# One upward tile per group of the small expert items multiplied as fp32 from where it landed

## The reference

```
logits = t @ router_w + router_b            # 256 tokens, 8 experts
top_vals, top_idx = top_k(logits, 2);  top_w = softmax(top_vals)
for e in range(8):
    y = (silu(t @ w_gate[e]) * (t @ w_up[e])) @ w_down[e]     # 1024 -> 3584 -> 1024
    out += gates[:, e] * y
```

## Time and profile before

| what | us |
|---|---|
| median of 3 runs | 2671.87 (2670.59 to 2681.54) |
| the profiled execution | 2670.39 |
| its span in the profile | 2668.6 |
| the mixture's stretch in it, about | 1647 to 2648 |

### The profile page before, as it was taken

How to read it: one execution, slowest core, us unless ns; L and a number is a source line. 1 busy time by engine, 2 the same in 40 slices (tenths; PEclk the granted TensorE clock), 3 DMA queues, 4 the chain that set the end, 5 groups by cost and what they waited for, 6 DMA issues and landing times.

```text
span 2668.6 us, 45484 instructions
## 1 busy us (share of the span) xinstructions
PE 2522.3 (95%) x17582; PEld 2135.5 (80%) x17601; DVE 2020.8 (76%) x1962; ACT 1497.9 (56%) x1519; POOL 89.3 (3%) x82
## 2 busy tenths in 40 slices
PE   8999999999999999999999999998899899888987
PEld 7888898888889898888889987776787678666855
DVE  6666877666666866667666756989888998998898
ACT  5443524445443515445446734678767776786676
POOL 6000006000000000000000000000000000000000
PEclk9999999999999999999999999999999999999998
DMA  8665313555564314564565413999999999999993
GB/s 280 191 183 178 117 35 127 189 189 175 190 208 144 101 35 158 189 200 159 189 189 156 149 47 120 381 349 362 366 349 343 366 366 347 351 371 334 326 367 142
DMA packets 342893, 601.45 MB, mean 225 GB/s; under 512 B 11984, under 2 KB 180816, under 8 KB 342608
## 3 DMA queue, kind: packets, MB, share of 16 engines
q1 hardware_dynamic: 335264, 590.85, 64.6%
q10 hardware_dynamic: 7472, 8.35, 0.9%
HBM read 598.11 MB, written 1.05 MB: 225 GB/s over the span
## 4 chain that ended last, share of the span: by engine, by line
DMA 34%; PE 34%; DVE 18%; DVEq 7%; ACT 4%; issue 2%; another core or an unknown queue 0%; ACTq 0%; SPq 0%; PEld 0%; PEldq 0%
DMA raw<-in_ffn_w_down 12%; DVE wlo L316 12%; PE ps L567 6%; DMA raw<-in_w_in 6%; DVEq L318 6%; DMA raw<-in_moe_w_up 5%; DMA work<-in_moe_w_gate 4%; PE ps L591 4%; PE ps L570 3%; ACT whi L312 3%; PE ps L2983 3%; PE ps L856 2%; PE ps L3027 2%; PE ps L2988 1%; DMA raw<-in_moe_w_gate 1%
## 5 line engine op out<-in xcount | busy, mean ns | idle before, releaser
L316 DVE TENSOR_TENSOR wlo<-raw,whi 128x2048 fp32r<-128x2048 f32 (+1 forms) x394 | 901.9, 2289 | 183.3 <-ACT whi L312 172.3
L312 ACT CAST whi<-raw 128x2048 fp32r<-128x2048 f32 (+1 forms) x394 | 751.4, 1909 | 380.9 <-DMA raw<-in_ffn_w_down 142.6
L567 PE MATMUL ps<-xboth,whi 128*128 128x512 f32 x1680 | 420.8, 392 | 0.0
L2983 PE MATMUL ps<-whi,xboth 128*128 128x512 f32 x1344 | 352.7, 398 | 5.1 <-issue 3.9
L567 PEld LDWEIGHTS ps<-xboth,whi 128*128 128x128 f32 x1680 | 305.3, 189 | 57.1
L2983 PEld LDWEIGHTS ps<-whi,xboth 128*128 128x128 f32 x1344 | 246.3, 188 | 59.0 <-issue 7.8
L316 DVE TENSOR_TENSOR wlo<-U,whi 128x2048 fp32r<-128x2048 f32 x112 | 256.2, 2287 | 25.2 <-ACT whi L312 18.3
L2988 PE MATMUL ps<-wlo,xboth 128*128 128x512 f32 x896 | 248.0, 399 | 15.1 <-DVE wlo L316 12.8
L312 ACT CAST whi<-U 128x2048 fp32r<-128x2048 f32 x112 | 213.7, 1912 | 54.1 <-DMA U<-in_moe_w_up 44.1
L570 PEld LDWEIGHTS ps<-xboth,wlo 128*128 128x128 f32 x1680 | 229.2, 190 | 16.4
L570 PE MATMUL ps<-xboth,wlo 128*128 128x256 f32 x1680 | 234.2, 282 | 0.0
(11 more groups left out here) (586 smaller groups left out, 3738.9 us busy)
## 6 DMA issues: line engine op xcount, KB each, us to landing
raw<-in_moe_w_gate SPq DMA_DIRECT2D x58, 1024.0 KB, 6.2
raw<-in_moe_w_up SPq DMA_DIRECT2D x56, 1024.0 KB, 6.8
U<-in_moe_w_up SPq DMA_DIRECT2D x56, 1024.0 KB, 6.8
U<-in_moe_w_down SPq DMA_DIRECT2D x56, 1024.0 KB, 6.4
raw<-in_ffn_w_gate SPq DMA_DIRECT2D x55, 1024.0 KB, 5.4
raw<-in_ffn_w_up SPq DMA_DIRECT2D x55, 1024.0 KB, 5.4
raw<-in_ffn_w_down SPq DMA_DIRECT2D x55, 1024.0 KB, 5.0
work<-in_moe_w_gate SPq DMA_DIRECT2D x54, 1024.0 KB, 6.5
```

Of the source, the lines that this page charges most:

```text
L312: act.copy(whi[:, n % SPLIT, 0:width], buf[:, 0:width]).then_inc(hi_ready[n % RAW], 1)
L316: dve.tensor_tensor(wlo[:, n % SPLIT, 0:width], buf[:, 0:width], whi[:, n % SPLIT, 0:width], ALU.subtract).then_inc(split_ready[n % SPLIT], 1)
L567: pe.matmul(ps[:, first_bank + b, :], whi[:, n % SPLIT, c * GW + b * P:c * GW + (b + 1) * P], xboth[:, c].rearrange("p a t -> p (a t)"), s ...
L2983: pe.matmul(dst, part[:, rows, xhalf(q)], whi[:, (m + k) % SPLIT, c * EW:(c + 1) * EW], start=(rows == 0 and part is xhi), stop=False)
```

## The change

In groups 1 to 6 of each small item the second upward tile (u1, called whole) gets no high and no low part. TensorE multiplies it as fp32 straight from its slot, with `x_whole`, an fp32 copy of the lower half of the gathered rows of 64 tokens (four blocks of 128 x 64) that ScalarE makes with four more activations in `gather_hi`. That is 24 of the 336 tiles. Its four fp32 matmuls go to the upper 64 rows of bank 6 and signal `whole_done`. The slot is given free by ScalarE after it has waited for `whole_done` and copied the low rows of up. The places of `whi` and `wlo` are counted over the tiles that are split (`count`, `place`), and `ahead` names the tile that goes into a place next: four tiles later rather than three where a whole tile lies between. So VectorE's list has five subtractions between two `turned`: `refill` for a0 now makes d0's part, for a1 d1's, for u0 that of the next a0, for u1 nothing, for d0 that of the next a1, for d1 that of the next u0.

```
-        def split_hi(act, n, width=TILE, landed=16, slot_of=raw_slot):
+        def split_hi(act, n, width=TILE, landed=16, slot_of=raw_slot, place=None):
...
-            act.copy(whi[:, n % SPLIT, 0:width], buf[:, 0:width]).then_inc(hi_ready[n % RAW], 1)
+            act.copy(whi[:, n % SPLIT if place is None else place, 0:width], buf[:, 0:width]).then_inc(hi_ready[n % RAW], 1)
...
+        x_whole = mt(4 * FEW).rearrange("p (c t) -> p c t", c=4)
+        f["whole_done"] = f["pool_u0"]
...
+        WHOLE = [ITEM_TILES + 6 * g + 3 for g in range(EN - 1)]
+
+        def parts_plan(n):
+            body = n + 4
+
+            def whole(m):
+                return m >= body and (m - body) % (2 * ITEM_TILES) in WHOLE
+
+            def count(m):
+                rounds, rest = divmod(max(m - body, 0), 2 * ITEM_TILES)
+                return m - rounds * len(WHOLE) - sum(w < rest for w in WHOLE)
+
+            def place(m):
+                return count(m) % SPLIT
+
+            def ahead(m):
+                t = m + SPLIT
+                while whole(t) or count(t) < count(m) + SPLIT:
+                    t += 1
+                return t
...
+            def as_it_came(m, dst):
+
+                buf, landed, _ = slot_of(m)
+                take(pe, landed, 16)
+                for c in range(C // 2):
+                    mm = pe.matmul(dst[0:FEW], x_whole[:, c, :], buf[:, c * EW:(c + 1) * EW], start=False,
+                                   stop=(c == C // 2 - 1), skip_group_check=True)
+                mm.then_inc(f["whole_done"], 1)
...
                 for k in range(2):
                     begin(k)
+                    if whole(m + k):
+                        as_it_came(m + k, dst)
+                        continue
...
-                    take(act, tile_done[(m + 1) % SPLIT])
-                    low_copy(6, "up_low")
-                    if m + 1 + SPLIT < end:
-                        split_hi(act, m + 1 + SPLIT, slot_of=slot_of)
+                    if whole(m + 1):
+                        take(act, f["whole_done"])
+                        low_copy(6, "up_low")
+                        act.sem_inc(slot_of(m + 1)[2], 1)
+                    else:
+                        take(act, tile_done[place(m + 1)])
+                        low_copy(6, "up_low")
+                        split_after(m + 1, end)
...
             def gather_hi(bank, b, q):
+                if q and b == 1:
+                    for c in range(4, C):
+                        act.activation(x_whole[:, c - 4, :], four(bank)[:, c % 4, 0:FEW], ACT.Copy, scale=moe_gain(c))
...
             def refill(m, end):
-                if m < end:
-                    dve.wait_ge(hi_ready[m % RAW], 1)
-                    split_lo(dve, m, slot_of=slot_of)
+                if not whole(m) and ahead(m) < end:
+                    dve.wait_ge(hi_ready[ahead(m) % RAW], 1)
+                    split_lo(dve, ahead(m), slot_of=slot_of, place=place(m))
```

More of the change, by code:

```diff
@@ L311, in split_hi, with split_lo @@
             act.sem_clear(here)
-            act.copy(whi[:, n % SPLIT, 0:width], buf[:, 0:width]).then_inc(hi_ready[n % RAW], 1)
-        def split_lo(dve, n, width=TILE, slot_of=raw_slot):
+            act.copy(whi[:, n % SPLIT if place is None else place, 0:width], buf[:, 0:width]).then_inc(hi_ready[n % RAW], 1)
+        def split_lo(dve, n, width=TILE, slot_of=raw_slot, place=None):
             buf, _, free_ = slot_of(n)
-            dve.tensor_tensor(wlo[:, n % SPLIT, 0:width], buf[:, 0:width], whi[:, n % SPLIT, 0:width],
-                              ALU.subtract).then_inc(split_ready[n % SPLIT], 1)
+            at = n % SPLIT if place is None else place
+            dve.tensor_tensor(wlo[:, at, 0:width], buf[:, 0:width], whi[:, at, 0:width],
+                              ALU.subtract).then_inc(split_ready[at], 1)
             dve.drain().then_inc(free_, 1)
@@ L542, in build, with take_split @@
         PASSES = ((whi, 0), (wlo, 0), (whi, 1))
-        def take_split(pe, n):
-            take(pe, split_ready[n % SPLIT])
+        def take_split(pe, n, place=None):
+            take(pe, split_ready[n % SPLIT if place is None else place])
         def wide_fresh(pe, n, first_bank):
@@ L2910, in blocks_of @@
             return ps[:, bank, :].rearrange("p (k t) -> p k t", t=P)
+        WHOLE = [ITEM_TILES + 6 * g + 3 for g in range(EN - 1)]
[13 more added lines that the diff above has]
+                return t
+            assert (2 * ITEM_TILES - len(WHOLE)) % SPLIT == 0
+            return whole, place, ahead
         def moe_stream(sp, n, l):
@@ L2962, in moe_tensor @@
             first_tiles = range(n, n + SPLIT)
+            slot_of = moe_slots(n)
+            whole, place, _ = parts_plan(n)
             def upper(m):
@@ L2982, in by_token @@
                         for part in ((xhi,) if q else (xhi, xlo)):
-                            pe.matmul(dst, part[:, rows, xhalf(q)], whi[:, (m + k) % SPLIT, c * EW:(c + 1) * EW],
+                            pe.matmul(dst, part[:, rows, xhalf(q)], whi[:, place(m + k), c * EW:(c + 1) * EW],
                                       start=(rows == 0 and part is xhi), stop=False)
@@ L2987, in by_token @@
                         rows = k * C // 2 + c
-                        mm = pe.matmul(dst, xhi[:, rows, xhalf(q)], wlo[:, (m + k) % SPLIT, c * EW:(c + 1) * EW],
-                                       start=False, stop=(rows == C - 1))
-                    mm.then_inc(tile_done[(m + k) % SPLIT], 1)
+                        mm = pe.matmul(dst, xhi[:, rows, xhalf(q)], wlo[:, place(m + k), c * EW:(c + 1) * EW],
+                                       start=False, stop=(rows == C - 1 or (c == C // 2 - 1 and whole(m + k + 1))))
+                    mm.then_inc(tile_done[place(m + k)], 1)
             def add_low(low, whole, bank):
@@ L3026, in downs @@
                             for part in ((hh,) if q else (hh, hl)):
-                                pe.matmul(ps[:, s, :], part[:, 2 * k + b, :], whi[:, (m + k) % SPLIT, cols_of(b, s)],
+                                pe.matmul(ps[:, s, :], part[:, 2 * k + b, :], whi[:, place(m + k), cols_of(b, s)],
                                           start=False, stop=False, skip_group_check=True)
@@ L3031, in downs @@
                         for b in range(2):
-                            mm = pe.matmul(ps[:, s, :], hh[:, 2 * k + b, :], wlo[:, (m + k) % SPLIT, cols_of(b, s)],
+                            mm = pe.matmul(ps[:, s, :], hh[:, 2 * k + b, :], wlo[:, place(m + k), cols_of(b, s)],
                                            start=False, stop=(final and k == 1 and b == 1), skip_group_check=True)
-                    mm.then_inc(tile_done[(m + k) % SPLIT], 1)
+                    mm.then_inc(tile_done[place(m + k)], 1)
                 if final:
@@ L3119, in moe_scalar, with split_after @@
             slot_of = moe_slots(n)
+            whole, place, ahead = parts_plan(n)
+            def split_after(m, end):
+                if ahead(m) < end:
+                    split_hi(act, ahead(m), slot_of=slot_of, place=place(m))
             def next_split(m, end):
-                take(act, tile_done[m % SPLIT])
-                if m + SPLIT < end:
-                    split_hi(act, m + SPLIT, slot_of=slot_of)
+                take(act, tile_done[place(m)])
+                split_after(m, end)
             def low_copy(bank, low):
@@ L3262, in item @@
             def item(m, q, i, end, last=False):
-                m += SPLIT
                 for g in range(1, EN):
@@ L3336, in moe_vector @@
             for k in range(4):
-                refill(n + SPLIT + k, open_end)
+                refill(n + k, open_end)
             make_hid(0, 0)
@@ L3347, in moe_vector @@
             turned(1)
-            refill(end - 1, end)
+            refill(end - 1 - SPLIT, end)
             for s in range(2):
```

7 lines of the change are left out of this document (3 added, 4 removed).

## The result

The changed kernel takes 2637.53 us (median of 4 runs, 2636.47 to 2637.74); the kernel before, run beside it, 2676.46 us (2670.59 to 2681.54). The ratio is 0.9861, 95% interval [0.9848, 0.9875]: about 37 us faster (the two medians lie 38.9 us apart). The forecast was 2645.3 us, 26.6 us faster, with a range of 2624 to 2671; it started from 2671.87, the median of the first three runs of the kernel before. The profiled execution took 2637.74 us, its span is 2635.9 us.

What follows compares the result with a forecast made beforehand. VectorE's list was taken to bound the small items, with a 15.39 us ring limiting the gain; 3 x 7.1 + 5.3 = 26.6 us off the median 2671.87 gave 2645.3 us, eight in ten 2624 to 2671.

Steps and rivals of the forecast that it cites:

- VectorE's list: Small items: VectorE's sequence of work sets the intervals of `turned`, 101.79 us an item before the change.
- 58 us: Small items: optimistic end, 24 removed subtractions of 2.43 us all gained on VectorE; not the forecast.
- The ring: Small-item groups: `turned` to d0, ScalarE's copy, VectorE's work to the next `turned`; 4.43 + 10.96, together 15.39 us.
- VectorE's idle time: Small-item groups after the change: VectorE idle about 2 us per group, ended by ScalarE's copy.
- the cap: Small items: the 15.39 us circuit of buffer places turns most of VectorE's removed 2.43 us per group into waiting.
- The sum over the items: Small items: 7.1 us in each of three and 5.3 us in the last, 26.6 us.
- Step: TensorE's fp32 whole tile: time between successive records, 0.43 to 0.45 us, eight records per group.
- cover: Small-item groups on TensorE: the fp32 tile ends 0.67 us before it would delay d0.
- The slower rival: Small items: fp32 tile delays d0; at 1.2 GHz throughout (7.0 us), +36 us in all, 2708; chance 0.07.
- The DMAs: Small items: rival that 369 GB/s bounds them, intervals stay 16.96, 2672 us; chance 0.18 including d0 delayed by the tile.
- the reserve: Small items: a loaded tile lies about 23 us before use, so later freeing of its slot costs 0.

Runs made afterwards that it cites:

- putting the load back: The changed kernel with VectorE making the low part of the next a0 twice in each group with a whole tile: 2667.35 us.
- the half tile: The changed kernel with two of the four fp32 matmuls of each whole tile left out: 2659.68 us.
- the second pair: The kernel before and the changed kernel, each profiled once more with no edit: 2673.77 and 2636.53 us.
- the kernel before with fillers: The kernel before with six bf16 matmuls of zeros ahead of TensorE's wait for `turned` in each small-item group: 2665.25 us, beside 2674.34.

## Why the prediction was right, and where its size was off

- *What bounds.* Before the change it is VectorE's list in small items: shown by putting the load back (items 94.8 to 101.0 us).
- *Not 58 us but 27.* The ring of d0, ScalarE's copy, four subtractions and `turned` was reckoned at 15.39 us; plain intervals are 15.36, in the change and at full clock in the half tile. VectorE's idle time appeared where it was put, 1.8 us for ScalarE's copy, and freeing `turned` from the second subtraction broke the cap.
- *The sum over the items.* Forecast 26.6 us; measured over the three full small items and five intervals of the last, first against first profile, 6.8 + 7.0 + 7.0 + 5.5 = 26.3 us.
- *What was missed.* The spans differ by 32.7 us in the first profiles and 37.2 in the second. Outside the items: 1.5 us in the kernel's last group, 2.8 to 3.0 at the loop's first return, 5.5 at leaving it, and 1.8 in an interval at the end of the last large item in the second pair only. Against these stand up to 1 us over the other intervals and the work ahead of the mixture, which the change doesn't touch: it took 2.9 us longer in the first pair and 0.4 in the second. The forecast had no term for these; it took everything outside the small items as unchanged. So the items came out to 0.3 us, and that the whole came out 6 to 11 us better has another source. Inside the large items the forecast held, to 0.2 us an interval: the interval in which ScalarE makes `x_whole` went from 18.66 to 18.84 us in the first pair and from 18.83 to 18.82 in the second.
- *TensorE.* Step 0.437 us (0.43 to 0.45 forecast); 0.47 us of cover instead of 0.67.
- *The slower rival* put the danger at the clock falling during the tile. The mechanism was nearer the opposite: the tile keeps the clock up, and with half of it there are 12 more half-clock stretches. Those that hit the ring lengthened an interval by 0.7 to 1.7 us each, and the small items by 11.1 us in all. That the change would end this risk was said only in half a sentence, and the sum had no term for it; the ring interval assumed a full clock and got it.
- *The DMAs.* 384 GB/s in the small item, above the 369 of before. The Trainium skill (Perfetto Trace Analysis, Engine Utilization) gives 358 GB/s per core as 100%, and says in the same section that this is the share with both cores of a pair active and that one core alone can draw more, up to some 120% of it. This trace agrees: one core works here, and 384 is 107%. So DMA bandwidth didn't bound the small item at 369, and the reserve of at least 13.5 us in that item shows that it doesn't at 384.

Open is why the loop's first return and its exit got cheaper. At the exit ScalarE's copy waits 6.1 us in the kernel before (6.6 in its second profile) and 0.8 in the change, with tiles long landed. The long branch also appears with VectorE's load kept (2.1 us) and with half the tile (6.2 us), and is short in six others, the kernel before with fillers among them. So it isn't tied to the new matmuls; its cause stays open, and no experiment here explains these 6 to 11 us of the gain.

## What to carry to other kernels

When work is taken from a full engine, follow the buffer places round: the place that the next piece of work needs is freed by a step that waits for that engine's own later output, and this ring gives the gain, not the engine's spared time. Then look for the cheapest link in the ring, here a short operation queued behind a long one that nobody waits for yet; moving it gave 15 us where the removed work had given 26. Time that another engine spends waiting isn't always free to leave empty: once TensorE is in the ring, filling its wait, even with zeros, was worth 9.5 us in the items by the clock.

## What the runs showed of the hardware that I had not expected

- Taking 1.7 us of matmuls out of each of 24 groups made the kernel 22 us slower, 11 us of it by the clock in the small items, and 1.8 us of zero products per group undid it. In those items the stretches at 1.2 GHz (3.4 us, once 6.8) began about where TensorE's wait for `turned`, of 2.0 to 2.9 us, ended (not at each such wait), and each lengthened its interval by 0.7 to 1.7 us, with TensorE in the ring. Where VectorE's list was the bound, those of an item together cost 0.4 us.
- A branch at the end of a loop can take TensorE's sequencer 0.4 us or 2.0 to 6.2 us in kernels that differ only in a few instructions of one engine; the kernel before and the change each showed the same in both of their profiles.
- An fp32 matmul of 128x64 by 128x512 is two records 0.437 us apart; its weight loads (137 ns) stayed hidden.
